# The last rows of a down stage and VectorE's search step, in the other order

## What is computed

```python
_, idx = lax.top_k(score, n_sel)                    # mixer B: the best 256 keys of each row
...
x = x + jnp.einsum('bsd,de->bse', merged, w_out[layer])
h2 = _rmsnorm(x, norm2_g[layer])
ff = jax.nn.silu(jnp.einsum('bsd,df->bsf', h2, w_ffn_gate[layer])) * jnp.einsum('bsd,df->bsf', h2, w_ffn_up[layer])
x = x + jnp.einsum('bsf,fd->bsd', ff, w_ffn_down[layer])
return _rmsnorm(x, norm_f_g)
```

## Time and profile before

| | us |
|---|---|
| median of 3 runs | 3094.03 |
| lowest, highest | 3092.43, 3094.33 |
| the profiled execution | 3094.78 |
| its span, from the first to the last instruction | 3093.0 |
| TensorE busy | 3033.4 (98%) |
| VectorE busy | 1826.1 (59%) |
| ScalarE busy | 1422.6 (46%) |
| GpSimd busy | 2024.6 (65%) |

### The profile page before, as it was taken

How to read it: one execution, slowest core, us unless ns; L and a number is a source line. 1 busy time by engine, 2 the same in 40 slices (tenths; PEclk the granted TensorE clock), 3 DMA queues, 4 the chain that set the end, 5 groups by cost and what they waited for, 6 DMA issues and landing times.

```text
span 3093.0 us, 44024 instructions
## 1 busy us (share of the span) xinstructions
PE 3033.4 (98%) x15678; PEld 2684.4 (87%) x15678; DVE 1826.1 (59%) x3706; ACT 1422.6 (46%) x2589; POOL 2024.6 (65%) x2201
## 2 busy tenths in 40 slices
PE   9999999999989999999999999999999999999998
PEld 8888888888878888898888888988888899888887
DVE  4236647637665556567776766967868689521111
ACT  3324535436463534346455534937655378420001
POOL 5666766665557677765677775376777922667777
PEclk9999999999999999999999999999999999999999
DMA  5766455355615333332533343163333510433333
GB/s 148 211 175 180 123 171 152 109 169 162 209 43 187 106 115 112 112 123 72 204 113 115 104 125 118 36 241 102 102 112 116 173 27 19 169 104 102 102 109 102
DMA packets 464201, 392.59 MB, mean 127 GB/s; under 512 B 29264, under 2 KB 394064, under 8 KB 463344
## 3 DMA queue, kind: packets, MB, share of 16 engines
q1 hardware_dynamic: 442544, 345.56, 37.1%
q10 hardware_dynamic: 21440, 44.22, 3.8%
HBM read 323.76 MB, written 62.81 MB: 125 GB/s over the span
## 4 chain that ended last, share of the span: by engine, by line
PE 80%; DVE 7%; ACT 5%; POOL 3%; issue 3%; DMA 2%; ACTq 0%; SPq 0%; DVEq 0%; POOLq 0%
PE BANK L1066 18%; PE BANK L1068 18%; PE BANK L1067 18%; PE BANK L1352 3%; PE LP L1066 3%; PE LP L1067 3%; PE LP L1068 3%; PE BANK L1377 2%; PE BANK L1379 2%; PE LP L1332 2%; PE LP L1333 2%; PE LP L1188 2%; PE LP L1187 2%; POOL WLO L1003 2%; DVE MASK L2094 1%
## 5 line engine op out<-in xcount | busy, mean ns | idle before, releaser
L1003 POOL TENSOR_TENSOR WLO<-WRAW,WHI 128x512 fp32r<-128x512 f32 x912 | 1209.9, 1327 | 76.1
L1001 POOL TENSOR_SCALAR WHI<-WRAW 128x512 fp32r<-128x512 f32 x912 | 632.4, 693 | 676.7 <-PE BANK L1068 518.7
L1066 PE MATMUL BANK<-H2hi,WHI 128*128 128x512 f32 x1376 | 524.6, 381 | 4.8 <-POOL WLO L1003 2.9
L1068 PE MATMUL BANK<-H2hi,WLO 128*128 128x512 f32 x1376 | 521.5, 379 | 0.0
L1067 PE MATMUL BANK<-H2lo,WHI 128*128 128x512 f32 x1376 | 521.5, 379 | 0.0
L1066 PE MATMUL BANK<-HThi,WHI 128*128 128x512 f32 (+1 forms) x1024 | 394.2, 385 | 0.9 <-DVE QS L2067 0.6
L1068 PE MATMUL BANK<-HThi,WLO 128*128 128x512 f32 (+1 forms) x1024 | 388.9, 380 | 0.0
L1067 PE MATMUL BANK<-HTlo,WHI 128*128 128x512 f32 (+1 forms) x1024 | 388.9, 380 | 0.0
L1773 ACT ACTIVATE MASK<-SCD,THR 128x896 bf16<-128x896 f32 (+5 forms) x186 | 282.2, 1518 | 195.0 <-DVE THR L2127 167.7
L1066 PEld LDWEIGHTS BANK<-H2hi,WHI 128*128 128x128 f32 x1376 | 260.1, 189 | 42.2 <-POOL WLO L1003 3.6
L1068 PEld LDWEIGHTS BANK<-H2hi,WLO 128*128 128x128 f32 x1376 | 260.0, 189 | 36.9
(11 more groups left out here) (314 smaller groups left out, 6456.8 us busy)
## 6 DMA issues: line engine op xcount, KB each, us to landing
WRAW<-in_w_in SPq DMA_DIRECT2D x124, 512.0 KB, 4.4
WRAW<-in_w_ffn_gate SPq DMA_DIRECT2D x88, 512.0 KB, 3.7
WRAW<-in_w_ffn_up SPq DMA_DIRECT2D x88, 512.0 KB, 3.8
WRAW<-in_w_ffn_down SPq DMA_DIRECT2D x88, 512.0 KB, 3.5
qsp<-QS SPq DMA_DIRECT2D x32, 512.0 KB, 5.7
WRAW<-in_w_out SPq DMA_DIRECT2D x32, 512.0 KB, 4.6
gates<-GS ACTq DMA_DIRECT2D x62, 256.0 KB, 2.3
GL<-gates ACTq DMA_DIRECT2D x48, 256.0 KB, 4.6
```

The costliest lines, as they stand in the source:

```text
L1001: nc.gpsimd.tensor_scalar(hi, raw, 1.0, 1.0, ALU.mult, ALU.mult).then_inc(w_hi, 1)
L1003: nc.gpsimd.tensor_tensor(lo, raw, hi.bitcast(f32), ALU.subtract).then_inc(w_split, 1)
L1066: nc.tensor.matmul(dst, whi, mhi, start=first, stop=False)
L1068: return nc.tensor.matmul(dst, wlo, mhi, start=False, stop=last)
```

## The change

In half 1 of the first two down stages VectorE now does its four additions first and its search step behind them. That concerns six places: two down stages in each of blocks 0, 1 and 2. In half 0, and in the third down stage, nothing changes, and no other engine's instructions change or move.

```diff
                     for half in range(D // ROWS):
-                        if half == 0 or part is not PARTS[-1]:
+                        if half == 0:
                             look("fd", part, half)
                         if half and part is PARTS[-1]:
                             half_mean(("fd", part[0]), 2)
...
                             if half and part is PARTS[-1] and b + 1 < NB and j < JT - 1:
                                 next(ahead[0])
+                        if half and part is not PARTS[-1]:
+                            look("fd", part, half)
                     before = ("fd", part[0])
```

## The result

| | before | after |
|---|---|---|
| median, us | 3094.18 (6 runs) | 3104.45 (6 runs) |
| ratio, 95% interval | | 1.0035, 1.0025 to 1.0045 |
| span of the profiled execution | 3093.0 | 3101.9 |

The forecast was 3097.3 us in a range of 3092.5 to 3099.5. The sign was right, the size was not, and the time lies outside the range. TensorE's granted clock has the same mean (0.997 in both). I had written that it is full throughout. It isn't quite: it falls for a few microseconds at several places, and not at the same ones in every execution (from 2103 to 2121 us it is 0.91 in the changed kernel's profiled execution and 1.00 in that of the kernel before).

A forecast was written before the change was run, and what follows sets the result against it. TensorE, busy 98% of the span, was taken as the bound. Terms +2.8 (block 2, second stage), +0.5 (its first stage) and 0 (blocks 0 and 1) gave +3.3 us, so 3097.3 us, range 3092.5 to 3099.5.

The forecast's parts named there:

- The wait for X goes: Block 2, second down stage: TensorE's 1.77 us wait for VectorE's additions to X disappears, -1.8 us for the first gate job.
- GpSimd gives the 1.8 us back: Block 2, second stage: TensorE, 1.8 us early, is caught by GpSimd's weight splits behind late scalings and loses the 1.8 us.
- The step's length in block 2 and the chain to the first product: Block 2, second stage: step lasts 10.8 us, ends at 2389.7; first product follows at 2395.7, 4.1 us late.
- Of the 4.1 us, 3.1 pass: Block 2, third part: the silu's 1.05 us lead absorbs some lateness, so the third product starts 3.1 us late, at 2417.2.
- The block's term: Block 2, second stage: TensorE later by 2.8 us at the last hidden low part; bounds -1.0 and 4.1 us.
- Blocks 0 and 1 cost nothing: Third term, 0, at most +0.5 us: block 1's 5.94 us idle before the third product; shorter counts elsewhere.
- Block 1's step kept at 7.0 us: Block 1, second stage: the step lasts 7.0 us with shorter counts; used for block 2's lower bound of 8.1 us.
- First stage of block 2, +0.5: Second term: maxima 1.7 us late for ScalarE, idle time takes half, the rest reaches TensorE through the near tile's low part.
- The first, a shorter step in the new place: First rival: step under 8 us in its new place, gain kept, end 1.0 us earlier, 3093.0 us; chance 0.20.
- the rule of the Trainium skill: Two-input VectorE and SBUF-reading GpSimd instructions exclude each other; the moved step would shed stretched instructions where GpSimd idles.
- The second rival: Lateness grows: three more GpSimd-VectorE meetings of 1.4 us in block 2's third part, +7.5 us, 3101.5 us; chance 0.10.
- Both marks that I had set for being wrong: Wrong if the time moves by over 6 us, or if the difference comes from block 0 or 1.

The follow-up runs named there:

- The divided step: Kernel before, with the four additions inside the long step in all second down stages, between last count and threshold correction: 3092.63 us, 0.9996; again 3093.70 us, 0.9992.
- the kernel before without counts: Kernel before, with the two counts of the long search step (line 2094) left out: 3092.55 us, ratio 0.9996.
- The doses: Changed kernel and kernel before with the long step's counts varied; changed kernel: 1.0000 without counts, 1.0025 with one, 1.0035 as it was, 1.0054 with three.
- the late start of the near pieces: Kernel before, with the first near piece of the second and third part begun two places later on TensorE: 3107.35 us, ratio 1.0043.
- one count: Changed kernel, with one of the long step's two counts (the fourth tile's) kept and the other left out: 3102.8 us, ratio 1.0025.
- the second stage of block 2 moved: Kernel before, with the changed order only in the second down stage of block 2: 3100.13 us, ratio 1.0020.
- three counts: Changed kernel, with the fourth tile's count made twice in the long step: 3111.05 us, ratio 1.0054.

## Why the forecast was wrong, point by point

- **The wait for X goes: right.** No such wait is left.
- **GpSimd gives the 1.8 us back: wrong as a rule.** The divided step and the kernel before without counts keep them whole. In the changed kernel they are lost, where it is late at the same time.
- **The step's length in block 2 and the chain to the first product: right.** 10.6 us for 10.8, 17.4 for 17.8. The scaling waited 3.7 us for 2.2, since TensorE and with it GpSimd came 1.8 us earlier, which I had not taken into the wait.
- **"Of the 4.1 us, 3.1 pass": the step that failed in block 2.** I went from the first product to the third with the lengths of the old trace, and took off the 1.05 us that the silu had ahead of it. Taking that off was right. What failed is that nothing was added: about 2 us were. Two of the instructions on the way, before and then after:

```profile
2393.58 0.58 DVE L2159 TENSOR_SCALAR EQD<-MASK 128x1664 bf16<-128x1664 bf16 x1
...
2406.81 0.29 DVE L2164 SCALAR_TENSOR_TENSOR NEED<-CSD,NEED 128x1 f32<-128x1 f32 x1
```

```profile
2401.76 1.47 DVE L2159 TENSOR_SCALAR EQD<-MASK 128x1664 bf16<-128x1664 bf16 x1
...
2416.10 1.22 DVE L2164 SCALAR_TENSOR_TENSOR NEED<-CSD,NEED 128x1 f32<-128x1 f32 x1
```

The first product is 3.7 us late. Between it and the second the mark of line 2159 takes 0.9 us more, the two scans 0.2 and line 2288 0.1, so the second is 4.9 us late (31.8 us behind the last down matmul for 27.0). Line 2164 takes 0.9 us more, so the silu ends 5.8 us late. Less its slack, the third product started at 41.0 us, against 36.2 before and 39.3 in the forecast: 4.8 us late; the sixth 5.5. The block's term was +2.8; the trace has 6.6 less 1.5 for the first stage, so 5.1.
- **Blocks 0 and 1 cost nothing: the larger failure.** They cost 0.5 and 3.1 us. In block 2 I had gone by the silu's slack; in block 1 I took VectorE's 5.94 us of idle time instead. The silu and the product there, before and then after:

```profile
1829.97 0.60 ACT L1996 ACTIVATE SL<-BANK 128x512 f32<-128x512 f32 x1
```

```profile
1836.06 0.60 ACT L1996 ACTIVATE SL<-BANK 128x512 f32<-128x512 f32 x1
...
1836.76 0.70 DVE L2549 TENSOR_TENSOR BANK<-BANK,SL 128x512 f32<-128x512 f32 x1 [3.30 <-ACT SL L1996]
```

The silu was only 2.7 us ahead of the product at 1833.31, and the third product came 4.1 us late (38.3 us behind the last down matmul for 34.2), released by the silu. Even so TensorE shows no wait for a product in this block. It waits for the near tile's low part, in the middle of its own gate job, 1.3 us, and for GpSimd. The view of its waits showed the first for block 2; that block 1 had no such wait meant only that there was slack, and I never asked how much. The doses put its end between 6.1 and 10.5 us, and the step ended at 11.4.
- **Block 1's step kept at 7.0 us: wrong.** It took 10.4. Six of its short instructions (lines 2127, 2134, 2136, 2140, 2142 and 2144) were held up beside GpSimd's splits, where it had been two (2140 and 2149). I had even used the 7.0 as the lower bound for block 2. With 7.0 us the step would have ended at 8.0 us; by the line of the doses, an estimate, that is just inside the slack, and my zero would have held.
- **First stage of block 2, +0.5: mechanism right, size off.** The wait for the near low part went from 0.9 to 2.4 us, +1.5.
- **The rivals.** The first, a shorter step in the new place, fell: 10.6 us for 10.8 in block 2, and 10.4 for 7.0 in block 1. I wrote that by the rule of the Trainium skill (page "SBUF — State Buffer", section "Who interferes with whom") the step would shed its stretched instructions where GpSimd is idle. The trace agrees with the rule's exclusion: the held instructions end within 0.03 us of GpSimd's. What failed was my reading that GpSimd is idle there; behind the down stage it begins the splits of the gate weights at the same bank release that VectorE's additions wait for. The second rival, lateness that grows by meetings, is nearest to what happened, for 0.10 of the chance. But it put three meetings of 1.4 us into block 2, where the trace shows about 2 us ahead of the third product, and not the 3.4 us of step length in block 1. A cost in block 1 stood in no rival. Both marks that I had set for being wrong are met: over 6 us, and a difference from block 1.

The sum by its terms: 0 became 0.5 and 3.1 us, 0.5 became 1.5, 2.8 became 5.1. That is 10.2 by one trace and 10.3 by the medians, where I had 3.3. That they agree so closely is partly chance, for a single fall of the clock moves a trace by 1.7 us.

That the loss in block 2 beyond the first product comes from meetings of GpSimd and VectorE alone is argued from the lengths of these instructions, and no run separates it. Why the late start of the near pieces costs as much as 13 us is open too. In its trace 7.5 us of it lie in block 2, with a granted clock of 0.79 from 2386 to 2394 us and again from 2470 to 2478, which makes 3.4 us.

## What to carry to other kernels

Before moving work behind a deadline, list every consumer behind it up to the bounding engine itself, and for each its slack, also where the profile shows no wait: no wait means slack of unknown size, and idle time on one path says nothing of the others. A dose, in which the moved piece is made shorter and longer, brackets that slack in two or three runs. If a long piece blocks a short urgent one, divide it at a place where its tail is cheap, rather than swap them.

## What the runs showed of the hardware

A small VectorE instruction that starts inside one of GpSimd's splits can be held until the split ends: 0.16 us becomes up to 1.25 us, and this holds for some instructions with one input too (line 2144, 1.13 us, from 1807.88 to 1809.01, beside a subtraction from 1807.70 to 1808.98). It depends on the instruction. From 1150 to 2560 us in the two traces, all 183 of lines 2120 and 2127 that started inside a split ended with it, within 0.04 us; none of the 17 reciprocals did, nor any of the 18 of line 2158, which has one input and one element per partition. So the length of a chain of short instructions depends on where GpSimd stands and isn't the sum of its parts: one count of 2.3 us taken away made the step 0.5 us shorter, both counts, 4.5 us, made it 5.5 us shorter, and one more made it 2.8 us longer.

TensorE's granted clock can fall behind its waits. Behind the waits of 1.1 and 2.0 us in block 2's third down stage it was 0.72 over 6 us, which is 1.7 us, in three kernels (the second stage of block 2 moved, one count, three counts), and 1.00 in the changed kernel's own profiled execution. So the price of one and the same wait differs from execution to execution.
